# Matmul operands and sums walked from the last column to the first, and operand rows shifted by multiples of 16 bytes

## What is computed

```python
for i in range(DEPTH):                       # DEPTH = 2, x: (1, 512, 1024) float32
    hn = rmsnorm(x, norm_mix_pre[i])
    m = mamba2_mixer(hn, ...) if i == 0 else diff_attention(hn, ...)
    x = x + rmsnorm(m, norm_mix_post[i])
    hn = rmsnorm(x, norm_ffn_pre[i])
    h = causal_dwconv(hn @ w_up[i], conv_w, conv_b)      # 1024 -> 2 * 2816
    gate, up = split(h)
    x = x + rmsnorm((silu(gate) * up) @ w_down[i], norm_ffn_post[i])
```

## Time and profile before

| | |
|---|---|
| time before, median of 2 runs | 1435.88 us (1435.57 to 1436.19) |
| the profiled execution's own time | 1436.27 us |
| its span, first to last instruction | 1434.5 us |
| TensorE busy | 1417.3 us, 99% of the span |
| weight loads busy | 1192.6 us, 83% |
| VectorE / ScalarE / GpSimd busy | 1027.8 / 621.3 / 112.9 us |
| granted TensorE clock, mean | 0.998 of full speed |

### The profile page before, as it was taken

One profiled execution on the slowest core, in us unless ns is written; L12 is line 12 of the kernel. 1 busy time (PEld: TensorE's weight loads), 2 busy tenths in 40 slices (PEclk: granted clock), 3 DMA queues, 4 the chain that ended last, 5 costly groups with the idle time before them and its releaser, 6 DMA issues.

```text
span 1434.5 us, 21763 instructions
## 1 busy us (share of the span) xinstructions
PE 1417.3 (99%) x7506; PEld 1192.6 (83%) x7506; DVE 1027.8 (72%) x1575; ACT 621.3 (43%) x1019; POOL 112.9 (8%) x85
## 2 busy tenths in 40 slices
PE   8999999999999999999999999999999999999997
PEld 6888888888889888888888977777798888888887
DVE  6998889899437888888623677778588888886123
ACT  6656555557334323323323446556563332323221
POOL 0000000000110000000011032321110000000111
PEclk9999999999999999999999999999999999999999
DMA  4433332432231232323233112121212222233331
GB/s 169 176 137 126 142 125 109 138 140 74 89 132 38 96 102 88 102 91 110 101 101 139 31 59 74 59 74 56 89 63 84 92 102 96 94 105 103 101 101 60
DMA packets 37445, 142.34 MB, mean 99 GB/s; under 512 B 4176, under 2 KB 6352, under 8 KB 35344
## 3 DMA queue, kind: packets, MB, share of 16 engines
q1 hardware_dynamic: 37392, 141.63, 28.8%
HBM read 139.38 MB, written 2.23 MB: 99 GB/s over the span
## 4 chain that ended last, share of the span: by engine, by line
PE 94%; DVE 3%; DMA 1%; ACT 1%; issue 1%; SPq 0%; POOL 0%; POOLq 0%; ACTq 0%
PE bank L468 20%; PE bank L470 20%; PE bank L469 20%; PE b_x L468 7%; PE b_x L470 7%; PE b_x L469 7%; PE b_norm L1647 1%; PE b_norm L489 1%; PE b_y L1080 1%; PE b_y L468 1%; PE b_y L470 1%; PE b_y L469 1%; PE b_cb L1607 1%; DVE hn_lo L823 1%; PE b_x L1092 1%; PE b_y L1597 1%
## 5 line engine op out<-in xcount | busy, mean ns | idle before, releaser
L416 ACT ACTIVATE w_hi<-raw 128x1024 fp32r<-128x1024 f32 (+1 forms) x201 | 222.9, 1109 | 406.3 <-PE bank L470 291.1
L431 DVE TENSOR_TENSOR w_lo<-raw,w_hi 128x1024 fp32r<-128x1024 f32 (+1 forms) x181 | 234.1, 1293 | 229.2 <-ACT w_hi L416 229.1
L468 PE MATMUL bank<-hn_hi,w_hi 128*128 128x512 f32 x848 | 335.9, 396 | 2.9 <-DVE hn_lo L804 1.6
L470 PE MATMUL bank<-hn_hi,w_lo 128*128 128x512 f32 x848 | 330.8, 390 | 0.0
L469 PE MATMUL bank<-hn_lo,w_hi 128*128 128x512 f32 x848 | 330.3, 389 | 0.0
L468 PEld LDWEIGHTS bank<-hn_hi,w_hi 128*128 128x128 f32 x848 | 159.3, 188 | 38.1 <-DVE w_lo L431 3.2
L470 PEld LDWEIGHTS bank<-hn_hi,w_lo 128*128 128x128 f32 x848 | 159.2, 188 | 33.9
L469 PEld LDWEIGHTS bank<-hn_lo,w_hi 128*128 128x128 f32 x848 | 159.4, 188 | 32.1
L468 PE MATMUL bank<-h_hi,w_hi 128*128 128x512 f32 (+1 forms) x352 | 127.9, 363 | 0.0
L470 PE MATMUL bank<-h_hi,w_lo 128*128 128x512 f32 (+1 forms) x352 | 127.6, 362 | 0.0
L469 PE MATMUL bank<-h_lo,w_hi 128*128 128x512 f32 (+1 forms) x352 | 127.6, 362 | 0.0
(11 more groups left out here) (326 smaller groups left out, 2476.7 us busy)
## 6 DMA issues: line engine op xcount, KB each, us to landing
raw<-w_up SPq DMA_DIRECT2D x80, 512.0 KB, 3.2
raw<-w_mix SPq DMA_DIRECT2D x48, 512.0 KB, 3.3
raw<-w_dn SPq DMA_DIRECT2D x32, 704.0 KB, 4.1
raw<-w_qkv SPq DMA_DIRECT2D x20, 512.0 KB, 3.2
acs_bc<-scratch SPq DMA_DIRECT2D x8, 1024.0 KB, 5.7
ecs_bc<-scratch SPq DMA_DIRECT2D x8, 1024.0 KB, 4.7
raw<-w_sout SPq DMA_DIRECT2D x16, 512.0 KB, 3.2
first_raw<-w_up SPq DMA_DIRECT2D x8, 512.0 KB, 6.4
```

The lines of the kernel that those rows point to most:

```text
L416: nc.scalar.activation(halves_of(ph, j if own else rep, own or first and j < 4)[0], raw_of(ph, rep, first and j < 4), ACT.Copy).then_inc(h ...
L431: nc.vector.tensor_tensor(lo, raw_of(ph, rep, first), hi.bitcast(F32), ALU.subtract).then_inc(lo_made, 1)
L468: nc.tensor.matmul(acc[:], wh, hi, start=first, stop=False)
L470: return nc.tensor.matmul(acc[:], wl, hi, start=False, stop=last)
```

## The change

Two things change.

1. In `product` the accumulator and both moving operands are taken with their columns in reverse: each matmul now begins at the last token and ends at the first, and its sums are written in the same order. The weight tiles and the results are the same. All products go through this, those over 256 columns too (each half is reversed within itself). The other matmuls keep their order.
2. Buffers move by multiples of 16 B (`LINE` is 4 floats). `w_hi` and `w_lo` are widened by 64 B a slot and start 16 B in. `y_*`, `h_*` and `o_*` are made by a new helper `rows`, which adds 128 B and starts 112, 96 and 80 B in. `ybuf`, which lies under `y_lo`, moves with it.

What this makes of the places, in bytes beyond those of before, worked out from the sizes: `w_hi` slots +16 and +80, `w_lo` slots +144 and +208, `hn_*` +256, `y_lo` +368, `y_hi` +496, `h_hi` +352, `h_lo` +480, `o_hi` +336, `o_lo` +464, the own weight buffers of the boundaries +512. Modulo 64 B the weights are at 16, `hn` and the own buffers at 0, `y` at 48, `h` at 32 and `o` at 16.

```diff
+LINE = 4
...
+        def rows(name, n, lead, dt=F32, scope=ctx):
+
+            return sb(name, [P, n * S + 8 * LINE], dt, scope)[:, lead * LINE:lead * LINE + n * S].rearrange(
+                "p (n s) -> p n s", n=n)
...
-        w_hi = sb("w_hi", [P, 2, UW], F32R)
-        w_lo = sb("w_lo", [P, 2, UW], F32R)
+        w_hi = sb("w_hi", [P, 2, UW + 4 * LINE], F32R)[:, :, LINE:LINE + UW]
+        w_lo = sb("w_lo", [P, 2, UW + 4 * LINE], F32R)[:, :, LINE:LINE + UW]
...
-                ybuf = sb("ybuf", [P, YC, S], scope=lap)
-            y_lo = sb("y_lo", [P, YC, S], F32R, scope=ssm)
+                ybuf = rows("ybuf", YC, 7, scope=lap)
+            y_lo = rows("y_lo", YC, 7, F32R, ssm)
...
-                sb("early_hi", [P, HG, S], scope=lap)
+                sb("early_hi", [P, HG * S + 8 * LINE], scope=lap)
...
-            y_hi = sb("y_hi", [P, YC, S], F32R, scope=ssm)
+            y_hi = rows("y_hi", YC, 7, F32R, ssm)
...
-            h_hi = sb("h_hi", [P, FC, S], F32R, scope=ffn)
-            h_lo = sb("h_lo", [P, FC, S], F32R, scope=ffn)
+            h_hi = rows("h_hi", FC, 6, F32R, ffn)
+            h_lo = rows("h_lo", FC, 6, F32R, ffn)
...
-            o_hi = sb("o_hi", [P, NH, S], F32R, scope=att)
-            o_lo = sb("o_lo", [P, NH, S], F32R, scope=att)
+            o_hi = rows("o_hi", NH, 5, F32R, att)
+            o_lo = rows("o_lo", NH, 5, F32R, att)
...
-            nc.tensor.matmul(acc[:], wh, hi, start=first, stop=False)
-            nc.tensor.matmul(acc[:], wh, lo, start=False, stop=False)
-            return nc.tensor.matmul(acc[:], wl, hi, start=False, stop=last)
+            acc, hi, lo = (columns[:, ::-1] for columns in (acc, hi, lo))
+            nc.tensor.matmul(acc, wh, hi, start=first, stop=False)
+            nc.tensor.matmul(acc, wh, lo, start=False, stop=False)
+            return nc.tensor.matmul(acc, wl, hi, start=False, stop=last)
```

## The result

| | before | after |
|---|---|---|
| median of the timed runs | 1435.88 us | 1466.18 us (1465.88 to 1466.47) |
| ratio after / before | | 1.0211, 95% interval 1.0167 to 1.0255 |
| span of the profiled execution | 1434.5 us | 1464.7 us |

The changed kernel is slower by 30.3 us. That it is slower is clear of the noise; whether by more than 2% is not. I had forecast 1388. The time lies in my range, and it is the one that I had worked out for the rival *The meetings get more frequent* (1465), but my likeliest case had the wrong sign.

The account below looks back on a forecast made before the run. TensorE's own pace was taken as the bound: 1436.3 - 51.4 (lower fee) + 3 (given back for DVE) = 1387.9, the runs' median 0.4 lower, stated as 1388 us. The range for 8 in 10 was 1366 to 1470.

Parts of the forecast that it names:

- The meetings get more frequent: Rival: in all products, row reads and weight loads meet more often, fee 18 ns throughout, 1465 us; chance 0.14.
- my likeliest case: The fee of the product instructions falls by most, giving 1371 to 1407 us; chance 0.48.
- What bounds the kernel: Whole kernel: only TensorE's own pace counts, busy 1417.3 of 1434.5 us, if the other engines keep up.
- The fee and its count: Each of 6192 product instructions pays 13.3 ns beyond its columns, whatever its length: 82.6 us, 5.8% of the span.
- a fee of 5: Reversed columns in all products: the fee falls from 13.3 to 5 ns, 6192 x 8.3 = 51.4 us off.
- the lower bound: Least fee for reversed products, from plain float32 matmuls: 2.7 ns, 65.6 us off.
- The explanation behind it: In the products, a matmul's row read and the next one's weight load from the same memory get in each other's way.
- Places moved: Buffers moved by 16 B steps: relative places can't all be best, one more reason for a fee of 5, not 2.7.
- What a faster TensorE runs into: In 80 to 360 us DVE has 6% spare, its chains end last at times: 3 us given back.
- That the fee stays: Rival: changing fp32r weights takes a fixed 13.3 ns, 1436 us, or 1419 with a small gain; stays or falls slightly: 0.29.
- Half pace: Rival: products of 512 columns start 430 ns apart; chance 0.09.

Follow-up runs that it names:

- the streams: Small kernels without the model, output a copy of x: streams of 48 or 60 matmuls; fp32r, 512 columns, equal places: 226.7 ns forward, 233.3 with rows read backward.

## Why the prediction was wrong

**What bounds the kernel** was right. The distances of the products carry +30.2 of the +30.2 us of span, the other PE instructions -0.1, and ACT and DVE only wait longer. The two levels of the granted clock are the 1.00 and 0.50 of the streams over 64 and 32 partitions. The 2.4 GHz of the prediction is my estimate, the 0.417 ns a column of the earlier trace rows taken as one cycle; the profiles give the clock as a share alone.

**The fee and its count** were right: 6192 instructions, 13.3 ns each at the unmoved places, the same for 512 and 256 columns. That it can move, because rows at unchanged addresses showed other fees, was right as well. The streams add that the fee does depend on the length: the numbers of columns in between cost up to 16.7, and 192 columns cost 31. So the sentence that it "does not depend on its length" holds for the two lengths of this kernel and not beyond.

**The failed step** is "I take a fee of 5, nearer the float32 rows, as two reads in one direction with fixed starts should seldom meet". At unmoved places the fee rose to 20.0 for 512 columns, in the kernel with reversed columns alone (233.3 in steady stretches) and in the streams with a reversed read alone. By that, 4800 x 6.67 = 32.0 us on for the long products and 1392 x 1.5 = 2.1 off for the short ones: about 30 us, where the run measured 26.6 and its product distances 26.3. Part of what is missing is that before's `hn` products stand at 227.3 on average, not at 226.7, for the beginnings after other matmuls. Two things had gone into that step. One was a picture of two reads in one direction, but no trace shows in which direction a load reads its tile. No run shows the fee of 5 either, or its 51.4 us: at unmoved places a reversed row pays 20.0 ns at 512 columns and 11.7 at 256. The other was the choice of the nearest row. I took the plain float32 matmuls, 2.7 ns, as the lower bound and leant towards it. They take 0.8333 ns a column and pay 2.5 in the streams, as bf16 does at 0.4167 ns a column. They were no neighbours of an fp32r row in what counted. The nearer rows were those of the same instruction after other matmuls, at 18: they lay on the side that came, though in part by luck, for they show how a stream at equal places begins and not a pace that it keeps.

**The explanation behind it** fell in a stronger form too. The fee is not in proportion to what the load reads: loads of 128 to 1 weight columns leave a backward stream at 233.3. Yet the tile's place moves the pace: alone it takes it from 226.7 to 233.4 in streams, and from 227.3 to 232.7 for `hn` in the kernel with the weights 8 lines further. Whether the load's read and the row's read meet at all is not shown.

**Places moved.** "If the relative place matters it can't be best for all of these" was right, and I drew the wrong conclusion from it ("one more reason to take 5 and not 2.7"). For 512 columns, before's arrangement, tile and row at equal places modulo 256 bytes and at an even line, at 226.7 ns, was beaten by none of the places tried; the moves alone cost 21.4 us. The right weight of that sentence was: what stands today is the aligned case, so a move can hardly win and can well lose. I had written the first half of it under the rival of the more frequent meetings, as an argument against it. My count of places modulo 64 bytes was wrong as well: by it `o` stands 0 lines from the weights, and with the places moved alone it ran at 231.3.

**What a faster TensorE runs into** (3 us given back by DVE) was never reached.

**The rivals.** That the fee stays was refuted: 20.0 and 13.3 differ in every long stretch. Half pace, at 0.09, was refuted: fp32r streams run at 233.3 ns with the row read backward and at 226.7 with the sum written backward, and bf16 ones at 215.8 with both. The rival of the more frequent meetings had a fee of 18 throughout and 1465 us. The measured mean, (1302.8 - 1272.6) / 6192 = 4.9 ns more, is a fee of 18.2. Its size was right on average, which is partly luck: the long products lost 6.6 ns each and the short ones gained 1.1. Its reason, more frequent meetings of two reads, is not shown: the streams tell where the 20 ns appear and not what they are. It had 0.14, and the rows of the same instruction spoke for it more than for the likeliest case.

**Still open:** what an fp32r row at a granted clock of 1.00 pays these 13.3, 16.7 or 20 ns for, and what in the work ahead picks one of two paces at a place 1 line off.

## What to carry to other kernels

When TensorE is the bound, take the distance between starts less the time of the columns (here 0.4167 ns each), for each shape, and multiply it by the count: here it is 82.6 of 1436 us, and it moves with addresses and direction while PE's busy share stays at 99%. What ran fastest here for fp32r rows of 512 columns, at 226.7 ns, was to read forward and let weight tiles and rows start at equal places modulo 256 bytes, at line 0, 2 or 6 of 16 bytes (at line 1, and read backward, it was 233.3); a spare buffer of 128 bytes put ahead of the weights costs 1.7% here. Try such a change first in a small kernel of streams, at the very places and in the very order of the kernel (0.9 ns off at most here), and after different beginnings, since one place can have two paces (226.7 and 233.3, with the tiles 1 line off).

## What the runs showed of the hardware that I had not expected

- The place of a weight tile against the row counts, nearly with a period of 16 lines of 16 bytes: 226.7 ns at 0 and 16 lines, 233.4 at 8, but 226.7 at 15 and 228.4 at 31; in the kernel 1436.06 us at 16 lines and 1460.65 at 8.
- At equal places a row read backward costs 6.7 ns at 512 columns (fee 20), nothing at 320 (13.3 both ways), and gains 1.6 at 256 (11.7).
- A sum written backward costs nothing: 1435.34 us, ratio 0.9998.
- bf16 matmuls of the same shape pay 2.5 ns (215.8), forward and backward. fp32r pays nothing at a granted clock of 0.50: 426.7 ns for 512 columns, which is 0.8333 a column.
- The granted clock stood at 1.00 in a stream over 64 partitions, fell to 0.50 in the stream over 32 that followed, with PE busy throughout, and rose to 1.00 again within the next stream over 128.
- With the tiles 1 line off, a stream keeps either 226.7 or 233.3 to its end, by what came before it. At equal places, with the rows at line 6, it comes to 226.7 within about ten matmuls.
